# Hybrid streaming encoder layer: sample keys masked one turn ahead, and a re-laid order of the steps within a turn

## The chip, the cores and the metric

One NeuronCore of one Trainium2 chip runs the whole program. The metric is the device time of one launch in microseconds (us). Engines are named as in the profile: PE (matmul), DVE (vector), ACT (scalar), POOL (GpSimd), SP (the queue that issues most DMAs). Each engine runs its own list of instructions strictly in the order in which it was written, and waits on semaphores; whatever stands behind a waiting instruction waits too.

## The reference

One layer of a streaming encoder over 1024 prompt tokens and 8 sample streams of 16 tokens. After a combined input projection there are two head groups: sparse attention (8 heads) and a gated delta rule (8 heads, chunks of 64). The part that the change concerns is the delta rule of a head, for the prompt and for the samples:

```python
a_mat = jnp.where(strict, jnp.einsum('bnhid,bnhjd->bnhij', kb, k) * decay, 0.0)
m_mat = a_mat + jnp.eye(chunk, dtype=f32)
sol = lax.linalg.triangular_solve(m_mat, rhs, left_side=True, lower=True, unit_diagonal=True)
u, w = sol[..., :DV], sol[..., DV:]
kd = k * jnp.exp(glast[..., None] - gc)[..., None]

def step(s, inp):
    u_n, w_n, qg_n, qk_n, kd_n, gl_n = inp
    v_new = u_n - jnp.einsum('bhcd,bhde->bhce', w_n, s)
    o = jnp.einsum('bhcd,bhde->bhce', qg_n, s) + jnp.einsum('bhij,bhje->bhie', qk_n, v_new)
    s = s * jnp.exp(gl_n)[..., None, None] + jnp.einsum('bhcd,bhce->bhde', kd_n, v_new)
    return s, o
```

and afterwards `o` is normalised per token, gated with SiLU(z) and goes to the output projection. The 8 samples have a state each, and their 8 x 16 tokens share one tile of 128 rows, so the update `kd^T v_new` has to be cut by sample.

## The kernel before

The program has stages one after the other: normalise the input, project (and select keys) in 61 blocks, prepare gates, then `run_heads`, then the attention of the samples, then the output projection. The change lies in `run_heads` alone, which takes some 870 us of the 3215.

`run_heads` works on three heads at a time. `whole_order` lists ten iterations (turns), i = -2 to 7; in turn i the chain of states of head i runs (steps M_ and S_ and O_), the solve and the attention of head i+1 (D_, A_), and convolution and norms of head i+2 (N_). `iteration(i)` gives every step a place between 0 and 1 with `spread(first, last, steps)` and sorts by it; every engine's `run` then emits, in that one sorted order, its own part of each step. So the numbers in `iteration` are not times: they fix the order in which each engine takes its work, and nothing else.

What a turn does, with the names that the prediction uses:

- **M_read, M_state** (8 tiles): PE multiplies with the state S, DVE forms `vn` and updates S and `o`. A strict chain from tile to tile. DVE's memset of S (L1498) begins it, and stands for the turn's start here.
- **S_state, S_turn, S_new, S_out**: the samples. PE multiplies the 8 states (L1366), ACT copies that out, PE turns it back, DVE forms `vn_sample` (L1514), ACT writes the first part of `o` (in S_new), PE adds the second part (L1377, into PSUM) and DVE sums both (L1519). Then POOL multiplies `vn_sample` by a mask of the samples into `vmask`, eight copies side by side (L1060), and PE multiplies `kd^T vmask` into two PSUM banks (L1381), which DVE adds to the sample states (L1522). L1381 waits for the mask and also for `o_ready`, that is for L1519.
- **O_square, O_norm, O_out**: ACT squares `o`, DVE sums and normalises, ACT takes the root between (L1189), DVE scales `o` (L1532), PE turns it in three groups (L1391).
- **D_keys** (POOL: keys and values times gates, then clears TU), **D_turn, D_gram** (gram matrices with decays, five pairs of tiles; DVE writes A), **D_out, D_base, D_back**: SP sends the 16x16 diagonal blocks of A to memory and back in another layout; POOL forms first the masked levels Bm (L1039, four multiplies), then inverts the blocks (30 small steps, `base`); SP brings the inverses back into TU with eight DMAs. **D_level** (8 levels of matmuls, PE L1293 is the first of each), **D_last**, **D_solve** (uw, for the next turn).
- **N_tap, N_conv, N_silu** (convolution of head i+2, nine DVE passes L1442, then SiLU on ACT), **N_turn** (nine tiles turned on PE, L1237), **N_squares, N_sum, N_norms, N_unit** (unit norms; their result starts the next turn's D_keys and D_turn).
- **A_logits, A_bias, A_exp, A_norm, A_turn_p, A_values, A_gate**: attention of head i+1 in 12 parts, 8 tiles of queries.

The shared buffer `vmask` carries three things one after the other: the copy of the sample state (`swq`, its first two tiles), the mask product, and the squares of `o`. ACT needs a table load when it changes between Exp, SiLU and Sqrt.

## Time and profile before

| | us |
|---|---|
| three runs: median | 3215.42 |
| three runs: lowest, highest | 3193.49, 3221.22 |
| profiled execution, its time | 3217.03 |
| its span (first to last instruction) | 3214.9 |
| PE / DVE / ACT / POOL busy over the span | 87% / 36% / 30% / 26% |
| mean granted clock of PE over the span | 0.918 |

The page of the profile cuts the span into 40 slices. PE is busy nine tenths or more in the projection and in the output projection, and between four and eight tenths in slices 23 to 33, where `run_heads` lies; there DVE and ACT are each busy about half of the time. A row of the timeline reads: start in us from the span's start, duration, engine, source line, operation, output <- inputs, shapes, count; a bracket at its end gives how long the engine stood idle before it and who ended that. Several equal instructions may be merged into one row (x4).

### The profile page before, as it was taken

What the parts mean: (1) busy time and instruction counts of PE and PEld (TensorE: products, weight loads), DVE (VectorE), ACT (ScalarE), POOL (GpSimd) and SP (SyncE); (2) the same over time, 40 slices, a digit from 0 to 9 for tenths busy, and PEclk for the clock granted to TensorE, in tenths of its full rate; (3) what the DMA queues carried; (4) which work ended last, traced back from release to release, by engine and by line L of the source; (5) the groups of instructions that cost most, each with busy time, mean ns of one, the idle gap of its engine ahead of it and who ended that gap; (6) DMA issues with size and microseconds to landing.
All of it is one profiled execution on the core that took longest, in us unless ns stands there. A gap on an engine that the chain in (4) does not pass through costs nothing. (4 is left out here: it accounts for less than half of the span.)

```text
span 3214.9 us, 39925 instructions
## 1 busy us (share of the span) xinstructions
PE 2807.4 (87%) x15333; PEld 2503.0 (78%) x15333; DVE 1163.1 (36%) x2044; ACT 957.4 (30%) x1662; POOL 844.0 (26%) x713
## 2 busy tenths in 40 slices
PE   4999899999999999999999458777777685799997
PEld 3999599798989989899999437666566563487875
DVE  7000100843818062250600256555665542304142
ACT  5111111313121121211211344655556542222221
POOL 6222012121211212112122132232331320255553
PEclk6999699999999989999999779988898895699998
DMA  3222122121221212222121411222122113446543
GB/s 130 66 64 64 39 64 73 49 69 54 65 68 53 72 50 63 67 65 73 59 64 59 139 49 46 68 77 60 37 67 68 55 42 84 166 145 221 169 177 124
DMA packets 301720, 259.02 MB, mean 81 GB/s; under 512 B 88232, under 2 KB 252176, under 8 KB 299152
## 3 DMA queue, kind: packets, MB, share of 16 engines
q1 hardware_dynamic: 291564, 212.35, 22.5%
q10 hardware_dynamic: 10048, 45.27, 3.5%
q8 instruction: 63, 1.03, 0.1%
q14 instruction: 45, 0.37, 0.0%
HBM read 192.25 MB, written 65.33 MB: 80 GB/s over the span
## 5 line engine op out<-in xcount | busy, mean ns | idle before, releaser
L394 PE MATMUL bank<-hH,wL 128*128 128x384 f32 (+1 forms) x2928 | 981.9, 335 | 14.9 <-POOL wL L311 14.9
L395 PE MATMUL bank<-hL,wH 128*128 128x384 f32 (+1 forms) x2928 | 980.5, 335 | 0.0
L396 PE MATMUL bank<-hH,wH 128*128 128x384 f32 (+1 forms) x2928 | 980.2, 335 | 0.0
L311 POOL TENSOR_TENSOR wL<-raw,wH 128x512 fp32r<-128x512 f32 x244 | 314.2, 1288 | 1390.3 <-ACT wH L328 1390.3
L394 PEld LDWEIGHTS bank<-hH,wL 128*128 128x128 f32 (+1 forms) x2928 | 550.3, 188 | 19.2 <-issue 18.5
L395 PEld LDWEIGHTS bank<-hL,wH 128*128 128x128 f32 (+1 forms) x2928 | 550.3, 188 | 0.8
L396 PEld LDWEIGHTS bank<-hH,wH 128*128 128x128 f32 (+1 forms) x2928 | 550.2, 188 | 0.7
L328 ACT ACTIVATE wH<-raw 128x512 fp32r<-128x512 f32 x244 | 154.2, 632 | 1020.2 <-PE bank L396 964.6
L1902 POOL TENSOR_TENSOR owL<-oraw,owH 128x2048 fp32r<-128x2048 f32 x48 | 225.5, 4699 | 268.2 <-ACT owH L1922 268.2
L506 DVE TENSOR_SCALAR score<-relued,w_idx 128x512 f32<-128x512 f32 (+3 forms) x10 | 7.8, 778 | 685.1 <-ACT relued L353 684.6
L1961 PE MATMUL ob<-owH,mL 128*128 128x512 f32 x576 | 227.8, 395 | 28.6 <-POOL owL L1902 28.6
L1962 PE MATMUL ob<-owL,mH 128*128 128x512 f32 x576 | 226.5, 393 | 0.0
L1963 PE MATMUL ob<-owH,mH 128*128 128x512 f32 x576 | 226.3, 393 | 0.0
L471 DVE MAX8 top<-score 128x8 f32<-128x1024 f32 (+6 forms) x200 | 175.3, 877 | 6.9
L339 ACT ACTIVATE ptbuf<-bank 128x384 f32<-128x384 f32 (+1 forms) x183 | 90.1, 492 | 288.4 <-PE bank L396 288.4
L472 DVE MATCH_REPLACE8 score<-top,score 128x1024 f32<-128x1024 f32 (+6 forms) x200 | 171.6, 858 | 0.0
L1922 ACT ACTIVATE owH<-oraw 128x2048 fp32r<-128x2048 f32 x48 | 91.8, 1914 | 236.0 <-PE ob L1963 215.2
L1961 PEld LDWEIGHTS ob<-owH,mL 128*128 128x128 f32 x576 | 109.6, 190 | 55.4 <-issue 31.8
L1963 PEld LDWEIGHTS ob<-owH,mH 128*128 128x128 f32 x576 | 109.5, 190 | 23.2
L1962 PEld LDWEIGHTS ob<-owL,mH 128*128 128x128 f32 x576 | 109.7, 190 | 22.5
L446 PE MATMUL bank<-region 64*128 64x512 f32 (+3 forms) x320 | 118.1, 591 | 6.1 <-ACT relued L353 5.9
L1442 DVE SCALAR_TENSOR_TENSOR y<-xc,keep_cw,y 128x1179 f32<-128x1179 f32 x72 | 113.0, 1572 | 11.2 <-ACT y L1069 9.9
(302 smaller groups left out, 3457.2 us busy)
## 6 DMA issues: line engine op xcount, KB each, us to landing
raw<-in_w_in SPq DMA_DIRECT2D x240, 256.0 KB, 2.8
oraw<-in_w_out SPq DMA_DIRECT2D x48, 1024.0 KB, 5.1
proj_scratch<-ptbuf ACTq DMA_DIRECT2D x60, 576.0 KB, 2.8
xc<-proj_scratch SPq DMA_DIRECT2D x8, 1536.0 KB, 7.7
mraw<-mix_scratch SPq DMA_DIRECT2D x12, 768.0 KB, 5.8
x<-in_x_prompt SPq DMA_DIRECT2D x8, 1024.0 KB, 4.8
out_y_prompt<-yv ACTq DMA_DIRECT2D x8, 1024.0 KB, 4.0
ox<-in_x_prompt SPq DMA_DIRECT2D x8, 768.0 KB, 6.6
```

The costliest lines, as they stand in the source:

```text
L311: pool.tensor_tensor(wL[c % 2][:, :, :], raw[c][:, :, :], wH[c % 2][:, :, :].bitcast(F32), ALU.subtract).then_inc(low_ready, 1)
L328: nc.scalar.activation(wH[c % 2][:, :, :], raw[c][:, :, :], ACT.Copy).then_inc(high_ready, 1)
L394: pe.matmul(o, low, hH[:, kk, tok], start=first, stop=False)
L395: pe.matmul(o, high, hL[:, kk, tok], start=False, stop=False)
L396: last = pe.matmul(o, high, hH[:, kk, tok], start=False, stop=end)
L446: pe.matmul(rel[u % BANKS_REL][:, 0:width], qi[i % 2][rows, hd // 2, :], kiT[rows, c:c + width], start=True, stop=True).then_inc(rel_done, 1)
L471: chain(nc.vector.max(top8[:, :], sc))
L472: chain(nc.vector.match_replace(out=sc, in_to_replace=top8[:, :], in_values=sc, imm_value=TAKEN))
L1902: pool.tensor_tensor(wL[n % 2][:, :, :], raw[n % 2][:, :, :], wH[n % 2][:, :, :].bitcast(F32), ALU.subtract).then_inc(low_ready, 1)
L1961: pe.matmul(o, mL[:, kk, a], wH[n % 2][:, k, :], start=first, stop=False)
L1962: pe.matmul(o, mH[:, kk, a], wL[n % 2][:, k, :], start=False, stop=False)
L1963: last = pe.matmul(o, mH[:, kk, a], wH[n % 2][:, k, :], start=False, stop=end)
```

## The change

The sample mask no longer multiplies `vn_sample`, late in the chain of its own turn, but the keys `kd` of the samples, in the turn before: step S_keys, on POOL, writes `kd_seg`. PE then multiplies each sample's masked keys with `vn_sample`: eight matmuls of 128 columns with stationary operands of their own, in place of two of 512 columns with one. `swq` gets a buffer of its own. On POOL the levels Bm move behind the inversion of the blocks. And the places in `iteration` are set anew: grams end at 0.22 instead of 0.26, states run to 0.42 instead of 0.36, samples and output steps follow closer, attention is stretched from 0.74 to 0.80, the levels lie at 0.56 to 0.80 instead of 0.55 to 0.86, N_turn ends at 0.80 and the norms lie at 0.80 to 0.95 instead of 0.90 to 1.0. DMA steps move with them; the load of x for head i+3 goes from 0.78 to 0.52.

```diff
-        placed += spread(0.0, 0.36, states) + spread(0.36, 0.52, sample) + spread(0.52, 0.66, out)
+        placed += spread(0.0, 0.42, states) + spread(0.42, 0.50, sample) + spread(0.50, 0.62, out)
...
-        placed += spread(0.66, 0.90, natural) + spread(0.90, 1.0, norms)
+        placed += spread(0.62, 0.80, natural) + spread(0.80, 0.95, norms)
...
-        vmask = sbt("vmask", [P, TILES, P])
+        kd_seg = sbt("kd_seg", [P, TILES, P])
         wq = sbt("wq", [P, DEC_B, 2, DEC_T])
-        swq = vmask[:, 0:2, :]
+        swq = sbt("swq", [P, 2, P])
...
                 def base(h, _k):
-                    wait(pool, a_ready, h, 5)
-                    for m in range(LEVELS):
...
                     wait(pool, blocks_in, h, 16)
                     w = base_w[:, 0, :, :]
...
                     pool.tensor_copy(base_w[:, 1, :, :], w.rearrange("p r c -> p c r")).then_inc(base_done.sem, 1)

-                def sample_mask(h, _k):
-                    wait(pool, sm_vn, h, 1)
-                    pool.tensor_tensor(vmask[:, 0:DEC_B, :], vn_sample.unsqueeze(1).to_broadcast([P, DEC_B, P]), K["segcol"][:, :].unsqueeze(2).to_broadcast([P, DEC_B, P]), ALU.mult).then_inc(sm_mask.sem, 1)
+                    wait(pool, a_ready, h, 5)
+                    for m in range(LEVELS):
+                        if m == 0:
+
+                            wait(pool, wt_done, h - 1, NS)
+                        for g in range(2):
+                            lo, hi = QUADS[g]
+                            pool.tensor_tensor(Bm[m][:, lo:hi, :], A[:, lo:hi, :], K["level"][:, m, :].unsqueeze(1).to_broadcast([P, hi - lo, P]), ALU.mult).then_inc(level_ready.sem, 1)
+
+                def sample_keys(h, _k):
+                    wait(pool, o_norms, h - 1, 1)
+                    wait(pool, sm_ds, h - 1, 3)
+                    pool.tensor_tensor(kd_seg[:, 0:DEC_B, :], kd[h % 2][:, NT, :].unsqueeze(1).to_broadcast([P, DEC_B, P]), K["segcol"][:, :].unsqueeze(2).to_broadcast([P, DEC_B, P]), ALU.mult).then_inc(sm_mask.sem, 1)
...
                     for half in range(2):
-                        pe.matmul(big[:, half, :], kd[h % 2][:, NT, :], vmask[:, 4 * half:4 * half + 4, :], start=True, stop=True).then_inc(sm_ds.sem, 1)
+                        for b in range(4):
+                            last = pe.matmul(big[:, half, b * P:(b + 1) * P], kd_seg[:, 4 * half + b, :], vn_sample, start=True, stop=True)
+                        last.then_inc(sm_ds.sem, 1)
```

**POOL, from the end of one inversion to the start of the next.** In these rows `de` are the blocks being inverted, `kbe`, `kd` and `vb` the keys and values of D_keys. Before:

```order
L1056 COPY de<-de 72x256
L1060 TENSOR_TENSOR vmask<-uw,keep_segcol 128x1024
L1023 TENSOR_TENSOR kbe<-nat,keep_gates 128x1152
L1024 TENSOR_TENSOR kd<-nat,keep_gates 128x1152
L1025 TENSOR_TENSOR vb<-nat,keep_gates 128x1152
L1029 MEMSET TU 128x2304
L1039 TENSOR_TENSOR Bm<-AQ,keep_level 128x512 x4
L1042 TENSOR_SCALAR de<-de 72x256
```

and now:

```order
L1048 COPY de<-de 72x256
L1057 TENSOR_TENSOR Bm<-AQ,keep_level 128x512 x4
L1062 TENSOR_TENSOR kd_seg<-kd,keep_segcol 128x1024
L1023 TENSOR_TENSOR kbe<-nat,keep_gates 128x1152
L1024 TENSOR_TENSOR kd<-nat,keep_gates 128x1152
L1025 TENSOR_TENSOR vb<-nat,keep_gates 128x1152
L1029 MEMSET TU 128x2304
L1034 TENSOR_SCALAR de<-de 72x256
```

The four multiplies for Bm went from ahead of the inversion to behind it, and the masking reads `kd` where it read `uw`.

**ACT, around the sample step, in a full turn.** `vmask`/`swq` in the first row is the copy of the sample state, `PT` an attention tile, `uw` with `keep_gates` the first part of `o` (the last such row is that of S_new), `y` the SiLU of the convolution (N_silu). Before:

```order
L1069 ACTIVATE vmask<-big 128x8x2x16
L1069 ACTIVATE PT<-big 128x512
L1069 ACTIVATE uw<-big,keep_gates 128x128
L1085 ACT_TABLE_LOAD
L1085 ACTIVATE y<-y 128x1024
L1069 ACTIVATE PT<-big 128x256
L1085 ACTIVATE y<-y 128x1024 x2
```

and now:

```order
L1071 ACTIVATE swq<-big 128x8x2x16
L1071 ACTIVATE PT<-big 128x512
L1087 ACT_TABLE_LOAD
L1087 ACTIVATE y<-y 128x1024 x2
L1071 ACTIVATE uw<-big,keep_gates 128x128
L1199 ACTIVATE zb<-zb 128x1152
L1087 ACTIVATE y<-y 128x1024
```

The copy of S_new moved behind a table load and two SiLUs.

**ACT, from the squares of `o` to the root.** `osq` is the root of O_norm, `lg` a row of attention logits (A_exp). Before:

```order
L1202 ACT_TABLE_LOAD
L1202 ACTIVATE lg,am<-lg,am 128x896
L1197 ACT_TABLE_LOAD
L1197 ACTIVATE zb<-zb 128x1152
L1185 ACTIVATE vmask<-uw 128x1152
L1189 ACT_TABLE_LOAD
L1189 ACTIVATE osq<-osq 128x9
```

and now:

```order
L1195 ACTIVATE za<-za 128x1024
L1187 ACTIVATE kd_seg<-uw 128x1152
L1204 ACT_TABLE_LOAD
L1204 ACTIVATE lg,am<-lg,am 128x896
L1191 ACT_TABLE_LOAD
L1191 ACTIVATE osq<-osq 128x9
```

An exponential with a table load of its own moved from ahead of the squares to between the squares and the root; one table load fewer stands in the piece.

## Rows read from the trace of the kernel before

**Rows 1.** Busy time by stretch; columns: stretch, length, each engine's busy time, clock, DMA.
```profile
1960.64:2561.47 600.83, 454.83 (x2988) 378.86 (x2988) 355.02 (x740) 331.50 (x654) 185.43 (x240) 0.89 0.21 59
...
2561.47:2643.91 82.44, 64.62 (x429) 53.89 (x429) 40.56 (x107) 34.49 (x78) 24.58 (x40) 0.90 0.15 41
```

**Rows 2.** Tile S (ns min/median/max, first to last start); timeline of DVE, two turns' starts.
```profile
L1498 DVE MEMSET S<- x8: 165/165/165, 1960.6 to 2643.9; 128x128 f32 x8
...
2161.80 0.17 DVE L1498 MEMSET S<- 128x128 f32 x1
...
2261.00 0.17 DVE L1498 MEMSET S<- 128x128 f32 x1
```

**Rows 3.** Timeline of PE in turn i = 2; its last row is turn i = 7.
```profile
2203.62 2.08 PE L1366 MATMUL big<-wq,Ss 128*128 128x32 f32 x16
...
2208.91 0.49 PE L1377 MATMUL big<-uw,AQ 128*128 128x128 f32 x2 [0.29 <-DVE uw L1514]
...
2217.92 3.55 PE L1381 MATMUL big<-vmask,kd 128*128 128x512 f32 x4 [8.53 <-POOL vmask L1060]
...
2224.24 0.61 PE L1293 MATMUL big<-TU,Bm 128*128 128x128 f32 x4
...
2227.04 0.66 PE L1391 MATMUL big<-ident,uw 128*128 128x128 f32 x4 [2.19 <-DVE uw L1532]
...
2251.16 0.55 PE L1237 MATMUL big<-ident,y 128*128 128x128 f32 x3
...
2669.57 3.78 PE L1381 MATMUL big<-vmask,kd 128*128 128x512 f32 x4 [1.18 <-POOL vmask L1060]
```

**Rows 4.** Line L1060, who waited for it: who, us in total, times.
```profile
  PE big L1381: 55.4, 8
```

**Rows 5.** Timeline of POOL in turn i = -1, then i = 2, then i = 6.
```profile
1895.64 8.61 POOL L1039 TENSOR_TENSOR Bm<-AQ,keep_level 128x512 f32<-128x512 f32 x4 [18.88 <-DVE AQ L1474]
...
2168.09 2.02 POOL L1029 MEMSET TU<- 128x2304 f32 x1
...
2192.87 7.47 POOL L1039 TENSOR_TENSOR Bm<-AQ,keep_level 128x512 f32<-128x512 f32 x4 [22.76 <-DVE AQ L1474]
...
2215.41 0.60 POOL L1056 COPY de<-de 72x256 f32<-72x256 f32 x1
...
2215.97 1.89 POOL L1060 TENSOR_TENSOR vmask<-uw,keep_segcol 128x1024 f32<-128x1024 f32 x1
...
2591.93 5.21 POOL L1039 TENSOR_TENSOR Bm<-AQ,keep_level 128x512 f32<-128x512 f32 x4 [22.15 <-DVE AQ L1474]
...
2598.55 0.85 POOL L1042 TENSOR_SCALAR de<-de 72x256 f32<-72x256 f32 x1 [1.41 <-DMA de<-base_a_scratch]
```

**Rows 6.** Timeline of ACT in turn i = 2.
```profile
2207.46 0.60 ACT L1069 ACTIVATE PT<-big 128x512 f32<-128x512 f32 x1 [1.35 <-PE big L1414]
...
2208.88 0.37 ACT L1069 ACTIVATE uw<-big,keep_gates 128x128 f32<-128x128 f32 x1 [0.82 <-DVE uw L1514]
...
2209.27 1.28 ACT L1085 ACT_TABLE_LOAD   x1
...
2211.79 1.99 ACT L1085 ACTIVATE y<-y 128x1024 f32<-128x1024 f32 x2
...
2216.45 1.04 ACT L1202 ACTIVATE lg<-lg,am 128x896 f32<-128x896 f32 x1
...
2221.57 1.16 ACT L1185 ACTIVATE vmask<-uw 128x1152 f32<-128x1152 f32 x1 [1.51 <-PE big L1381]
...
2252.63 2.12 ACT L1104 ACTIVATE y<-nat 128x2304 f32<-128x2304 f32 x1
```

**Rows 7.** Line L1442 (min/median/max ns); timeline of DVE in turn i = 2.
```profile
L1442 DVE SCALAR_TENSOR_TENSOR y<-xc,keep_cw,y x72: 1435/1442/2562, 1837.2 to 2507.1; 128x1179 f32<-128x1179 f32 x72
...
2167.72 2.44 DVE L1435 COPY xc<-keep_cw 128x72 f32<-128x72 f32 x1
...
2225.62 1.36 DVE L1532 TENSOR_TENSOR uw<-uw,osq 128x1152 f32<-128x1152 f32 x1 [0.28 <-ACT osq L1189]
```

More of the change, by code:

```diff
@@ L782, in iteration @@
         solves = [("D_solve", h, g) for g in range(5)]
-        placed += spread(0.0, 0.07, turns) + spread(0.07, 0.26, grams) + [(0.265, ("D_out", h, 0)), (0.29, ("D_base", h, 0)), (0.42, ("D_back", h, 0))]
-        placed += spread(0.55, 0.86, levels) + spread(0.86, 0.92, [("D_last", h, q) for q in range(3)]) + spread(0.92, 1.0, solves)
+        placed += spread(0.0, 0.05, turns) + spread(0.05, 0.22, grams) + [(0.225, ("D_out", h, 0)), (0.24, ("D_base", h, 0)), (0.38, ("D_back", h, 0)), (0.57, ("S_keys", h, 0))]
+        placed += spread(0.56, 0.80, levels) + spread(0.80, 0.86, [("D_last", h, q) for q in range(3)]) + spread(0.88, 0.98, solves)
         attend = []
@@ L1031, in base @@
                 def base(h, _k):
-                    wait(pool, a_ready, h, 5)
-                    for m in range(LEVELS):
-                        if m == 0:
-                            wait(pool, wt_done, h - 1, NS)
-                        for g in range(2):
-                            lo, hi = QUADS[g]
-                            pool.tensor_tensor(Bm[m][:, lo:hi, :], A[:, lo:hi, :], K["level"][:, m, :].unsqueeze(1).to_broadcast([P, hi - lo, P]), ALU.mult).then_inc(level_ready.sem, 1)
                     wait(pool, blocks_in, h, 16)
@@ L1170, in sample_state @@
                     wait(act, sm_done, h, 1)
-                    copy(swq.rearrange("p n (b t) -> p b n t", b=DEC_B), big[:, 0, 0:2 * P].rearrange("p (b n t) -> p b n t", b=DEC_B, n=2)).then_inc(sm_out.sem, 1)
+                    copy(swq[:, :, :].rearrange("p n (b t) -> p b n t", b=DEC_B), big[:, 0, 0:2 * P].rearrange("p (b n t) -> p b n t", b=DEC_B, n=2)).then_inc(sm_out.sem, 1)
                 def state(h, t):
@@ L1184, in square @@
                     wait(act, sm_ds, h, 3)
-                    do(vmask[:, :, :], o, ACT.Square).then_inc(o_squares.sem, 1)
+                    do(kd_seg[:, :, :], o, ACT.Square).then_inc(o_squares.sem, 1)
                 def out_root(h, _k):
```

22 lines of the change are left out of this document (11 added, 11 removed).

## Prediction

> **What bounds the kernel now.** I read the stretches first. `run_heads` has eight memsets of S, one at the start of each turn i = 0 to 7, from 1960.6 to 2643.9 [rows 2]; six full turns lie between 1960.64 and 2561.47, 600.83 us or 100.1 each, and turn 6 takes 82.4 [rows 1]. In the full turns PE is busy 455 of 601 us, DVE 355, ACT 332, POOL 185: no engine is full, so a turn is as long as its longest chain through the five fixed lists, and a stall counts only if it lies on that chain.
>
> Next the timeline of PE in turn i = 2, which runs from 2161.80 to 2261.00 [rows 2]. S_state ends at 2205.70 (2203.62 + 2.08), the first part of the sample output starts at 2208.91, and then PE stands 8.53 us until 2217.92, for POOL's mask [rows 3]. All eight such waits sum to 55.4 us [rows 4]. POOL's timeline says why the mask is late: it ran 2215.97 to 2217.86, directly behind the last step of the inversion (2215.41 + 0.60); the inversion began when the four Bm multiplies ended at 2200.34, and those began at 2192.87, when the last gram was written [rows 5]. The mask stands in POOL's list behind work it has nothing to do with. Behind PE's wait stand L1381, D_level's first matmul at 2224.24 and O_out at 2227.04, again after 2.19 us of waiting [rows 3]; from O_out PE has work to the last N_turn, which ends at 2251.71, and 9.3 us later the next turn starts [rows 2, 3]. So the chain of a turn today is: grams, Bm, inversion, mask, L1381, squares, norm, O_out, levels with N_turn, norms of head i+2, next turn.
>
> **The change, step by step, for a full turn.** I put the times against the end of S_state, s = 2205.70.
>
> (1) *The mask leaves the chain.* L1381 then waits for L1519 only, and L1519 for ACT's copy in S_new. Today that copy stands directly behind an attention copy (2208.88); now a table load and two SiLUs come first. From s: the hand-off, the copy of the sample state and the attention tile (0.60, ending 2.4 after s today, about 1.35 when PE turns that tile right behind S_state), table load 1.28, two SiLUs 1.99, the copy 0.37 [rows 6], DVE's sum and the hand-off about 0.3. That is 5.3 after s, bounded by 4.9 and 6.3. Today L1381 starts 12.2 after s. Gain 6.9. A new wait of about 2 to 3 us on PE stays, ended by ACT.
>
> (2) *The mask itself* is the same size (128 x 1024) on POOL, 1.89 us [rows 5], now behind Bm and long before its use in the next turn: nothing, covered by POOL's idle time (it is busy 185 of 601 us [rows 1]). Without that cover it would cost 1.89.
>
> (3) *L1381 itself*: 2 matmuls x 512 columns become 8 x 128, the same 1024 columns (each runs as two passes), but with a weight load for each. No row shows this shape. Below it stands L1366, sixteen passes with own weights in 2.08 us, above it today's 3.55 [rows 3]; I take 3.55, no change, since columns and passes are equal and PE comes out of a wait as it does now.
>
> (4) *From L1381 to O_out.* Today 9.12 us (2217.92 to 2227.04) [rows 3]. Now an Exp with its table load stands on ACT between the squares and the root: L1381 3.55, squares 1.16, load 1.28, Exp 1.04, load 1.28, then root, the scaling on DVE 1.36 [rows 3, 6, 7] and hand-offs of about 0.7 give 10.4. Cost 1.3, bounds 0 (if ACT reaches the Exp early) and 2.3 (load and Exp in full).
>
> (5) *s moves.* DVE's list now puts convolutions 6 and 7 ahead of the last M_state instead of behind it: 2 x 1.44. Against it, today one convolution beside the Bm multiplies took 2.56 instead of 1.44 [rows 7], which goes as Bm moves behind the convolutions. Net +1.8; the grams are packed earlier, which lets M run a little freer; I take +1.2, bounds 0 and 3.
>
> (6) *The other chain, grams to levels.* With Bm out of the way the inversion starts when its blocks have come back. Turn 6 shows that time: Bm starts 2591.93, the inversion at 2598.55 after waiting 1.41 us for the DMA: 6.6 instead of 7.5 [rows 5]. Then the inversion as now, 15.7 (2200.34 to 2216.01), and at most 8.2 to the first level (2216.01 to 2224.24) [rows 3, 5]: grams + 30.5. If the grams ended no earlier than now (31.1 into the turn), the first level could start 61.6 in; by (1) to (5) O_out, which stands ahead of it in PE's new list, starts 65.2 - 6.9 + 1.3 + 1.2 = 60.8 in. So this chain follows close behind. Three fewer half-steps of M and one convolution fewer stand ahead of the last gram in the new lists; I expect the grams 1 to 3 us earlier, which makes O_out the later one. Bm runs beside the DMAs that bring the inverses back, 5.2 to 7.5 against 8.2.
>
> (7) *O_out to the last N_turn*: 24.7 today. The new list has one logits part, one turn and one level more behind O_out, and gets rid of short waits of about the same sum. Zero, bounds +-1.5.
>
> (8) *The border.* Norms still begin with the squares behind the last N_turn, since N_turn stands between the levels on PE. The new lists put D_last's copy ahead of the squares (2.12 [rows 6]) and one of D_last's subtractions between the sums: +0.7, bounds 0 and 2.1. N_pads goes ahead of the first update of S. Today this small copy took 2.44 us in turn 2, until POOL's memset of TU was over (2168.09 + 2.02) [rows 5, 7]. In the new place it would wait for the same end: nothing more, since in most turns the scaling ahead of it is held to that end already.
>
> (9) *DMAs.* The load of x is issued some 20 us earlier, behind the inverses and the sample store; its reader comes only in the next turn. The waiting SP holds back only stores. Zero. `swq` in its own buffer: zero.
>
> Sum for a full turn: -6.9 + 1.3 + 1.2 + 0 + 0.7 = -3.7; I take **-3.4**, since (6) is near. Turn 6 has no SiLUs and no norms but the chain of (6) alone; I give it the same. Turn 7 loses its wait of 1.18 [rows 3]; turn -1 starts its inversion up to 2.0 earlier (Bm took 8.61 there against 6.6 [rows 5]), I take 1.5. Together 7 x 3.4 + 1.2 + 1.5 = 26.5 us. The profiled execution took 3217.0 (span 3214.9 and 2.1 around it), 1.6 more than the median of 3215.4: 3190.5 for it, **3189** against the median.
>
> **Two rules of the Trainium skill.** Of table loads the rows show 1.28 us: the load ends at 2210.55 and the second SiLU starts at 2211.79 [rows 6], so one SiLU of about 1.0 lies between and nothing more. The Trainium skill's page "ScalarE: Activation LUTs", section "What ACT_TABLE_LOAD costs", adds a drain of 1.38 us to each load. By the page, (4) would be 2 x 1.38 = 2.8 us dearer, and the time 7 x 0.6 + 2.7 = 7 us below today's, 3208. The trace does not agree, as there is no room for a drain; I give that no chance of its own. The other rule is the second rival's.
>
> **Rivals.**
> *A: the whole wait comes back.* s doesn't move, the exponential is not in the way and the grams end 3 us earlier: 6.5 a turn, 7 x 6.5 + 2.7 = 48 us, 3167. For it: the mask wait is the one long stall of PE, and turn 6's Bm at 5.21 shows that POOL is faster when undisturbed [rows 5]. Against it: (4) and (6).
> *B: POOL holds DVE in O_norm.* Bm (5.2 to 7.5) and the new mask 1.89 now run directly behind the inversion, while DVE normalises `o` with a small scaling from SBUF to SBUF. The copy of N_pads, 2.44 us until POOL's run ended, is such a hold [rows 5, 7]. If the scaling is held to the mask's end, the turn loses about 1.9 more: -1.5, in all 13 us, 3202. The Trainium skill's page "SBUF — State Buffer", section "Who interferes with whom", says that DVE's two-port modes and POOL lock each other out for a whole instruction; N_pads agrees. Against: the root waits for ACT's table load anyway, some 1.5 us.
> *C: slower.* The states are stretched from 0.36 to 0.42 of the turn. If S_state's end followed its place, it would go from 43.9 in (2205.70 - 2161.80) to 51.2, 7.3 later instead of 1.2: +2.7 a turn, 7 x 2.7 - 2.7 = 16 us, 3231. It decides from 4.6 later on (3.4 + 1.2). Against: DVE's work ahead of it grows by 1.8, no more.
>
> **How the numbers follow.** Forecast (3175 to 3203) 0.50, A 0.26, B 0.14, C 0.10. About 1% (32 us, 3183) is what a measurement of this kernel can tell from no change. Faster by over 1%: A and a third of the forecast, 0.42. Slower by over 1% needs C with a shift of 9 and more: 0.06. Within 1%: 0.52. The range leaves out the far half of A and most of C: 3156 to 3212.
>
> **What would show it.** L1381's successor starts 5 to 6 us after S_state, released by ACT or DVE and not POOL; the inversion starts 6.6 after the last gram; O_out about 61 into the turn; about 10 from the last N_turn to the next memset; turns of 96 to 97. I am wrong if S_state ends later than 47 in, if DVE's scaling in O_norm shows a duration far over 0.2, or if PE waits for the inverses rather than for O_out.

## The result, and the profile after

The changed kernel takes 3174.4 us (median of 4 runs, 3163.9 to 3179.5), the kernel before 3208.7 in the runs beside it: ratio 0.9867, with a 95% interval of 0.9842 to 0.9893 (the quotient of the two medians is 0.9893, the upper end of it). It is 1.1 to 1.6% faster; the forecast was 3189 with "within 1%" as the likeliest case. The direction is right, the time lies in the range of 3156 to 3212, and the wait for the mask went as forecast. But the gain is larger, because the forecast had one term with the wrong sign: S_state's end, which came earlier and not later.

The profiled execution has a span of 3174.0 against 3214.9. The stretches of the changed kernel's trace that answer to [rows 1] (the six full turns, then turn 6; columns as there):

```profile
1958.18:2528.55 570.37, 457.78 (x3042) 393.28 (x3060) 347.62 (x741) 320.97 (x649) 165.60 (x241) 0.89 0.22 62
2528.55:2605.01 76.46, 61.10 (x438) 51.95 (x441) 43.14 (x106) 35.67 (x80) 24.10 (x40) 0.93 0.16 43
```

Six turns take 570.37 instead of 600.83, 95.1 instead of 100.1 each: 5.1 less, where 3.4 was forecast. Turn 6 is 6.0 shorter, also for 3.4. PE is busy as long as before (458 and 455): nothing was saved, only waiting.

PE in turn i = 2 of the changed kernel, which runs from 2148.54 to 2244.13 (start, duration, engine, line, tiles, idle time before and what ended it); the rows answer to [rows 3]:

```profile
2189.11 1.94 PE L1368 MATMUL big<-wq,Ss 128*128 128x32 f32 x16 [0.85 <-DVE S L1512]
...
2192.82 0.39 PE L1379 MATMUL big<-uw,AQ 128*128 128x128 f32 x2
2196.26 2.69 PE L1384 MATMUL big<-uw,kd_seg 128*128 128x128 f32 x16 [3.05 <-DVE uw L1523]
...
2206.61 1.11 PE L1395 MATMUL big<-ident,uw 128*128 128x128 f32 x4 [5.36 <-DVE uw L1536]
2207.52 1.06 PE L1295 MATMUL big<-TU,Bm 128*128 128x128 f32 x4
...
2231.39 0.49 PE L1239 MATMUL big<-ident,y 128*128 128x128 f32 x3
...
2235.24 1.11 PE L1325 MATMUL big<-WT,TU 64*64 64x64 f32 x8 [1.61 <-ACT WT L1071]
2236.86 0.79 PE L1338 MATMUL big<-vb,TU 128*128 128x128 f32 x2 [0.51 <-DVE TU L1497]
2237.45 0.63 PE L1339 MATMUL big<-TU,kbe 128*128 128x128 f32 x2
```

S_state ends at 2191.05 (2189.11 + 1.94), 42.5 into the turn. The main sample matmul (L1384) follows 5.2 later, released by DVE's sum and not by POOL: the wait of 8.53 in [rows 3] is gone, one of 3.05 is left. But before O_out (L1395) PE now stands 5.36. Over the whole program the waits for that scaling of `o` are the largest of this stretch (who waited at line L1395: who, us in total, times):

```profile
  DVE uw L1536: 89.2, 16
```

(L1395 is counted twice there, for its matmuls and for its weight loads; half of it, 45 us, is PE's.)

The table puts the segments of a turn side by side, as means over the six full turns, in us from the memset of S, the turn's start. Each is read from the timelines' rows: last gram written, end of S_state, start of the main sample matmul, start of O_out, start of the first level, end of the last N_turn, next memset.

| | grams | S_state's end | sample matmul | O_out | first level | N_turn's end | turn |
|---|---|---|---|---|---|---|---|
| before | 32.4 | 45.3 | 57.5 | 66.7 | 64.0 | 90.8 | 100.1 |
| after | 27.1 | 42.5 | 47.9 | 58.0 | 58.9 | 83.3 | 95.1 |
| segment, measured | -5.2 | -2.8 | -6.8 | +0.9 | | +1.2 | +2.5 |
| segment, forecast | -1 to -3 | +1.2 | -6.9 | +1.3 | | 0 | +0.7 |

(The segments run from S_state's end to the sample matmul, O_out, the last N_turn and the next memset: -2.8 - 6.8 + 0.9 + 1.2 + 2.5 = -5.0, and -5.1 without rounding.) Two terms lie outside their bounds: S_state comes 4.0 earlier than forecast, and the border from N_turn to the next turn costs 1.8 more.

### The profile page after: what moved, and what is told of

Its sections match the earlier page's. It is cut to its first block and busy times, and to the rows that moved or that the text cites. A ratio compares the mean times of both kernels' runs of the same rounds, so it can differ in the third digit from the quotient of the medians.

```text
span 3174.0 us, 40095 instructions
## 1 busy us (share of the span) xinstructions
PE 2804.9 (88%) x15405; PEld 2516.8 (79%) x15429; DVE 1156.2 (36%) x2044; ACT 948.0 (30%) x1657; POOL 819.6 (26%) x713
## 5 line engine op out<-in xcount | busy, mean ns | idle before, releaser
L1965 PE MATMUL ob<-owH,mL 128*128 128x512 f32 x576 | 227.0, 394 | 28.6 <-POOL owL L1906 28.6
L1993 DVE TENSOR_TENSOR yv<-ob,ox 128x512 f32<-128x512 f32 x36 | 22.6, 685 | 257.6 <-PE ob L1967 257.6
```

Of the source, the lines that this page charges most:

```text
L1965: pe.matmul(o, mL[:, kk, a], wH[n % 2][:, k, :], start=first, stop=False)
```

## Each part alone, and two parts undone

All figures are means over six full turns of the profiled execution, as in the table; ratios are to the kernel before, run beside each (its medians there were 3212 to 3218). Total times carry chance: two executions of the one changed kernel are 19 us apart (1826.6 and 1807.2) already at the first copy of N_pads, where `run_heads` has only begun. So the turns are compared first. The code changes are shown shortened: `...` stands for what is left out, and words behind `#` explain and are not in the code.

**The mask's step alone.** The kernel before, with the old table and Bm ahead, takes the keys' mask, the eight small matmuls and `swq`:

```
-  "S_new": sample_mask          # vmask = vn_sample x segcol, behind the inversion
+  "S_keys": sample_keys         # kd_seg = kd x segcol, at 0.57 of the turn before
```

> The kernel before with the mask step alone: keys masked in their own step ahead of time (kd_seg, S_keys at 0.57, 8 matmuls of 128 columns, swq apart), the old table of places, Bm ahead of the inversion as before. Theory T (the mask's gain needs the earlier grams): POOL's mask no longer stands between S_state and the main sample matmul, which starts 3.5 to 5.5 us behind S_state's end instead of 12.2; but the grams end where they did (32.4 into a turn), so the first level stays at about 64, and O_out, which stands behind it on PE, moves only from 66.7 to 65 to 66. Turns 1 to 2 us shorter, in all 8 to 14 us: 3195 to 3201 beside 3208.7. Rival R (the mask carries the gain alone): O_out 5 us earlier, turns of 95, 3174.

Measured 3208.6, ratio 0.9988 (0.9967 to 1.0009). The sample matmul comes 5.1 behind S_state, yet the way from there to O_out takes 15.7 instead of 9.2: O_out at 64.8. PE in its turn i = 2 says why:

```profile
2208.64 2.94 PE L1384 MATMUL big<-uw,kd_seg 128*128 128x128 f32 x16 [0.47 <-DVE uw L1523]
...
2222.18 1.22 PE L1295 MATMUL big<-TU,Bm 128*128 128x128 f32 x4 [3.92 <-DMA TU<-base_w_scratch]
```

The next wait is 3.92 us for the inverses coming back by DMA. The mask's wait, the longest of PE, was worth 0.5 us of a turn by itself, less than theory T's 1 to 2 and far from rival R's 5: the other chain (grams, inversion, levels) lay directly behind it.

**The new table alone**, with the old mask behind the inversion and Bm ahead of it:

> The new table of places alone: the mask stays on the sample's values behind the inversion, Bm ahead of the inversion, 2 matmuls of 512 columns, as before. Theory T: grams end at 27 into a turn, the inversion ends 7.5 + 15 later at 49.7, mask 1.9, main sample matmul at 52 instead of 57.5, O_out at 62, last N_turn 25 later, border 11.8: turns of 99, 1 us shorter than before, about 7 us in all: 3202. If the order carries the gain alone (rival O): turns of 95, 3174. If it gives nothing without the mask's step (rival R): 3207 to 3212.

Measured 3207.5, ratio 0.9973 (0.9949 to 0.9998). Grams at 26.4, inversion to 49.9, sample matmul at 51.8, O_out at 62.1, turns of 99.0: the theory's numbers. Neither part is measured at more than 0.3% alone; both together make 0.8% (the next run, where only Bm's move is missing), and with Bm's move 1.3%.

**Bm back ahead of the inversion**, everything else as changed:

```
+                    wait(pool, a_ready, h, 5)
+                    for m in range(LEVELS):          # the four Bm multiplies
...
                     wait(pool, blocks_in, h, 16)     # inversion
...
-                    wait(pool, a_ready, h, 5)
-                    for m in range(LEVELS):
```

> The changed kernel with the four Bm multiplies put back ahead of the inversion. Theory T: the inversion starts about 1 us later behind the grams, the first level at 60 instead of 58.9, O_out unmoved at 58 or a little earlier, since in turns 2, 4 and 6 DVE's small scaling in O_norm (2.72, 2.13 and 5.77 us instead of 0.17) is no longer held by Bm: within 5 us of the changed kernel either way, 3170 to 3179. Rival S (S_state came early because Bm no longer runs beside the convolutions): S_state's end 1.5 to 3 us later in each turn, time 3185 to 3195.

Measured 3187.1, ratio 0.9919 (0.9892 to 0.9945). Rival S is right: grams at 26.9, nearly as in the changed kernel (27.1), but S_state's end at 44.9 instead of 42.5. DVE, then POOL, in its turn 2:

```profile
2182.17 2.21 DVE L1446 SCALAR_TENSOR_TENSOR y<-xc,keep_cw,y 128x1179 f32<-128x1179 f32 x1
...
2184.49 1.36 DVE L1573 TENSOR_SCALAR lg<-lg,am 128x640 f32<-128x640 f32 x1
...
2186.43 1.79 DVE L1446 SCALAR_TENSOR_TENSOR y<-xc,keep_cw,y 128x1179 f32<-128x1179 f32 x1
```

```profile
2181.87 7.48 POOL L1039 TENSOR_TENSOR Bm<-AQ,keep_level 128x512 f32<-128x512 f32 x4 [19.59 <-DVE AQ L1478]
```

Beside Bm (2181.87 to 2189.35) a convolution takes 2.21 and the next 1.79 instead of 1.44, and the small scaling of the attention 1.36 instead of 0.55 (both in the changed kernel). The forecast had counted one convolution of 2.56 [rows 7].

**The grams at their old places**, everything else as changed:

```
-  spread(0.0, 0.05, turns) + spread(0.05, 0.22, grams) + [(0.225, D_out), (0.24, D_base), (0.38, D_back), ...
+  spread(0.0, 0.07, turns) + spread(0.07, 0.26, grams) + [(0.265, D_out), (0.29, D_base), (0.42, D_back), ...
```

> The changed kernel with D_turn, D_gram, D_out, D_base and D_back at their old places (0 to 0.07, 0.07 to 0.26, 0.265, 0.29, 0.42), all else as changed. Theory T (grams packed into the first fifth are what moves both the levels and S_state): grams end at 31 to 32, the first level at 62 to 63, O_out no longer the later one; S_state's end back at 44 to 45; turns 2.5 to 4 us longer than the changed kernel's 95.1, 3192 to 3200. Rival S (S_state came early through Bm's move or the convolutions' places): S_state's end stays at 42 to 43, turns longer by 2.5 at most through the levels.

Measured 3211.1, ratio 0.9993 (0.9977 to 1.0009): the whole gain is gone. Grams at 33.0, S_state's end at 45.7, O_out at 62.5. But a row of DVE, 4.06 into its turn 2, spoils the reading:

```profile
2160.06 4.12 DVE L1573 TENSOR_SCALAR lg<-lg,am 128x128 f32<-128x128 f32 x1
2162.15 2.08 DVE L1439 COPY xc<-keep_cw 128x72 f32<-128x72 f32 x1
```

A_norm's scaling of 128 x 128 takes 0.29 in the changed kernel and 4.12 here (3.7 to 4.1 in every turn). That hold is looked at below, and this run repeated without it.

## What bounds the turn of the changed kernel

**The state chain unstretched.**

```
-  spread(0.0, 0.42, states) + spread(0.42, 0.50, sample)
+  spread(0.0, 0.36, states) + spread(0.38, 0.52, sample)
```

> The changed kernel with the state chain back in the first 0.36 of a turn (sample from 0.38 to 0.52), so that each half-step stands ahead of a convolution or a gram that it now follows. Theory T (stretching the states did cost S_state some 4 us, as rival C had it, and packed grams and the move of Bm paid for it): S_state's end at 38 to 40 instead of 42.4, the grams 0.5 to 1.5 later, O_out held by the squares' chain or the inverses: turns within 1.5 us, 3165 to 3182. Rival: the stretch cost nothing; S_state stays at 42 to 43.

Measured 3190.3, ratio 0.9930 (0.9893 to 0.9968): slower than the changed kernel. S_state's end came at 41.3, only 1.2 earlier, and the grams at 28.6. A_norm's first scaling was held 3.7 in every full turn here too, and O_norm's 4.2 to 5.2. Neither side's number came out, so this run doesn't price the stretch.

**D_last ahead of the squares at the border.** This looks at the 11.8 us from the last N_turn to the next memset, 9.3 before. Turn 2 from O_out to the last N_turn, and from there to the next memset, for the kernel before and then for the changed one (windows, columns as in [rows 1]):

```profile
2227.04:2251.71 24.67, 23.24 (x184) 21.34 (x185) 10.47 (x20) 11.05 (x23) 0.00 (x0) 0.93 0.50 144
2251.71:2261.00 9.29, 6.37 (x63) 5.96 (x63) 6.66 (x9) 7.09 (x12) 0.00 (x0) 1.00 0.31 114
```

```profile
2206.61:2231.88 25.27, 24.60 (x186) 22.41 (x188) 10.49 (x22) 11.30 (x24) 0.00 (x0) 0.91 0.57 167
2231.88:2244.13 12.25, 9.82 (x72) 9.21 (x71) 7.57 (x14) 7.45 (x13) 0.51 (x1) 0.72 0.11 43
```

The border ran at full clock (1.00) before; after, 0.72 was granted. ACT's timeline of the changed kernel has the squares of N_squares ahead of D_last's second copy (WT):

```profile
2232.81 2.12 ACT L1106 ACTIVATE y<-nat 128x2304 f32<-128x2304 f32 x1
2234.83 0.36 ACT L1071 ACTIVATE WT<-big 64x256 f32<-64x256 f32 x1
```

PE waits 1.61 for that copy (the row of 2235.24 above), and D_solve's products of two passes then take 0.63 (the row of 2237.45): granted 0.50 from 2235.24 to 2241.71, the lower of the two clock levels, 1.2 GHz, which begins in that wait. In the next run, where PE doesn't wait there, they take 0.39, at 2.4 GHz (granted 1.00). But turn 5 of the changed kernel has the same wait of 1.61, and there the clock stayed up:

```profile
2518.71:2528.55 9.84, 7.14 (x72) 6.56 (x71) 7.39 (x14) 7.23 (x13) 0.12 (x1) 1.00 0.14 55
```

So with the wait and the full clock the border takes 9.8, 0.5 more than before; in the other five turns it takes 11.4 to 12.5, granted 0.72 to 0.85, and some 2 of the 2.5 is the clock. Why it fell in five borders and not in the sixth, no run shows.

```
-  spread(0.80, 0.86, [("D_last", h, q) for q in range(3)])  ...  spread(0.80, 0.95, norms)
+  spread(0.800, 0.806, [("D_last", h, q) for q in range(3)])  ...  spread(0.807, 0.94, norms)
```

> The changed kernel with D_last's three parts ahead of N_squares on ACT and DVE (places 0.800 to 0.806, norms from 0.807). Theory T (the border is 11.8 us and not 9.3 because the squares, 2.12 us, stand ahead of D_last's second copy, and D_solve ends after the norms): PE's wait of 1.61 us ahead of D_last's second product goes, D_solve starts 1.5 us earlier, N_turn's end to the next memset 9.8 to 10.5; six borders, 8 to 12 us: 3163 to 3167. Rival N (the norms are the later chain): border 11.3 or more, 3171 to 3175.

Measured 3177.4, ratio 0.9883 (0.9837 to 0.9930). PE at the start of D_solve in its turn 2:

```profile
2233.60 0.49 PE L1338 MATMUL big<-vb,TU 128*128 128x128 f32 x2 [0.51 <-DVE TU L1497]
2233.93 0.39 PE L1339 MATMUL big<-TU,kbe 128*128 128x128 f32 x2
```

The border fell to 10.2, as theory T has it, but for another reason: PE now stands 2.05 a little later, for ACT's copy of `uw`, and what is gained is the clock (0.94 to 1.00 in all six borders). Yet the time did not follow: S_state's end went from 42.5 to 43.5, and turn 6 from 76.5 to 81.4, where A_norm's scaling was held 4.18.

**The SiLUs behind O_norm.** ACT in turn 2 of the changed kernel has no gap from 2191.56 to 2204.15: table load, SiLUs, squares, table load, exponential, table load. Three of its rows:

```profile
2195.37 0.35 ACT L1071 ACTIVATE uw<-big,keep_gates 128x128 f32<-128x128 f32 x1
...
2199.25 1.16 ACT L1187 ACTIVATE kd_seg<-uw 128x1152 f32<-128x1152 f32 x1
...
2204.95 0.21 ACT L1191 ACTIVATE osq<-osq 128x9 f32<-128x9 f32 x1 [0.80 <-DVE osq L1534]
```

```
-  spread(0.45, 0.49, gates) ...  (0.47, O_silu)
+  spread(0.54, 0.56, gates) ...  (0.5395, O_silu);  A_bias part 9 at 0.4695, A_exp 6 at 0.4705
```

> The changed kernel with ACT's SiLUs (N_silu, A_silu, O_silu) behind O_norm, and the logits' part 9 and exponential 6 next to S_new, so that no SiLU and only one table load stand on ACT between S_state and the root. Theory T (ACT bounds the stretch from S_state to O_out, and the inverses stand close behind): main sample matmul 3 to 3.5 behind S_state instead of 5.6, O_out 4 to 5 earlier, 53 to 54 into the turn; the first level then waits for the inverses until 57.5 to 59, so turns shrink by 1 to 2 only: 3160 to 3167. Rival A (O_out alone bounds, the inverses have room): turns shrink by 4: 3146. Rival Z (the late SiLUs hold up the first levels' copies on ACT): same or slower, 3174 to 3185.

Measured 3167.4, ratio 0.9853 (0.9800 to 0.9907). The sample matmul comes 4.0 behind S_state, but O_out only at 57.1, 11.7 behind the matmul instead of 10.1. DVE and POOL of its turn 2:

```profile
2194.85 1.35 DVE L1533 TENSOR_REDUCE osq<-kd_seg 128x9 f32<-128x1152 f32 x1
2196.24 2.83 DVE L1535 TENSOR_SCALAR osq<-osq 128x9 f32<-128x9 f32 x1
```

```profile
2192.24 4.94 POOL L1060 TENSOR_TENSOR Bm<-AQ,keep_level 128x512 f32<-128x512 f32 x4
2197.13 1.90 POOL L1065 TENSOR_TENSOR kd_seg<-kd,keep_segcol 128x1024 f32<-128x1024 f32 x1
```

O_norm's scaling of 128 x 9 numbers lasts 2.83 (5.33 in four of the six full turns) and ends when POOL's S_keys ends, at 2199.03. That is rival B's mechanism, and here it is the bound (the run that splits Bm, below, takes most of it away and has O_out 3.1 earlier than the same kernel without the split).

**S_keys later.** In the changed kernel itself O_norm's scaling lasted 2.72, 2.13 and 5.77 in turns 2, 4 and 6, else 0.17.

```
-                    wait(pool, o_norms, h - 1, 1)
+                    wait(pool, o_norms, h - 1, 3)
```

> The changed kernel, where POOL's S_keys waits for the third step of O_norm (the reciprocal) instead of the first, so that it can't run while DVE's small scaling stands there. Theory B (the scaling is held by POOL's run of Bm and S_keys): its duration, 2.72, 2.13 and 5.77 us in turns 2, 4 and 6 of the changed kernel and 0.17 in the others, falls to 1.0 at most in turns 2 and 4, and to 3.9 in turn 6, where Bm itself still holds it; ACT's root then waits 0.8, 0.35 and 1.9 us less: 3 us in all, 3170 to 3175, too little for the time and read in the trace. Rival: the long scalings have another cause; then they stay.

Measured 3174.2, ratio 0.9879 (0.9832 to 0.9927). The scaling took 1.0 at most in the full turns and 3.97 in turn 6, where ACT's root waited 2.37 instead of 4.18. With Bm ahead of the inversion (the run above) it took 0.17 in all eight turns, though S_keys runs there too: the hold comes with Bm's new place.

**N_pads later; four moves; three moves.**

```
-  spread(0.03, 0.08, taps) + spread(0.08, 0.45, conv)
+  spread(0.093, 0.113, taps) + spread(0.113, 0.45, conv)
```

> The changed kernel with N_pads and the taps at 0.093 to 0.113 (behind M_state.1) instead of 0.03 to 0.08. Theory H (the small copy of N_pads on DVE is held until one of POOL's D_keys instructions ends, 2.12 us or 4.06 us from the same start, and the state chain and the grams stand behind it: grams at 25.3 or 27.2): the copy falls to 0.2 to 1.5 us, M_state.1 at 8.6 at the latest, grams at 25.5 or less in every turn; 1.5 to 2 us in most turns, 3160 to 3168. Rival V (another small instruction of DVE is held in its place, A_norm.1 above all): grams stay at 27, 3170 to 3178.

> The changed kernel with four small moves together: S_keys behind O_norm's reciprocal, D_last ahead of N_squares, SiLUs behind O_norm, N_pads behind M_state.1. Theory T (each has its place on the chain, and what the first three met alone was POOL's hold of DVE): grams at 25, DVE's scaling in O_norm under 1 us, O_out at 53 to 54, first level at 55.5 to 56.5 by the inverses, border 10.1: turns of 90 to 91.5 instead of 95.1, in all 25 to 32 us: 3142 to 3150. Rival (the gains overlap, or the inverses bind): turns of 93, 3160.

> As the one with four moves, without D_last ahead of N_squares. Theory T: border 11.8 instead of 10.1, turns 1.6 longer: 3152 to 3160. Rival V (without the later border, POOL's D_keys start 0.5 ahead of the memset and hold nothing; with it, they start later against the memset, hold DVE longer and give the border's gain back): this one is no slower than the one with four moves.

Measured 3175.6 (ratio 0.9896, 0.9838 to 0.9953), 3173.1 (0.9888, 0.9836 to 0.9940) and 3177.2 (0.9889, 0.9834 to 0.9945). With N_pads late the grams end at 25.3 to 25.7 in every turn, as theory H has it, but S_state's end is 43.4. The taps and convolutions stand later there, among the state steps; that this is why was not tried. With four moves five turns take 92.2 to 92.9 and one 97.6, and there A_norm's scaling was held 4.15. By the turns D_last's move is worth 2.1 (93.4 with it, 95.5 in the run of three moves, without it). But turn 6 takes 81.3 with it, where that scaling was held 4.15 again, and 76.8 without, and the two ratios don't tell the runs apart. So rival V is neither shown nor refuted. By the ratios none of the three beats the changed kernel. With four moves a hold took back part of the gain; with N_pads late the three small instructions took no more than 1.2 in a full turn, so there the reason is another and open.

## The hold of DVE by POOL

DVE's timeline of the changed kernel: the copy of N_pads in turn 2, O_norm's scaling in turn 2, the copy in turn 3:

```profile
2152.26 4.06 DVE L1439 COPY xc<-keep_cw 128x72 f32<-128x72 f32 x1
...
2201.95 2.72 DVE L1532 TENSOR_SCALAR osq<-osq 128x9 f32<-128x9 f32 x1
...
2247.84 2.12 DVE L1439 COPY xc<-keep_cw 128x72 f32<-128x72 f32 x1
```

The copy of 128 x 72 numbers starts 3.71 or 3.72 into both turns; it takes 4.06 in one and 2.12 in the other. POOL runs four instructions of about 2.1 back to back there (three multiplies of D_keys, then the memset of TU), and both ends are ends of such an instruction: of the memset in turn 2 and of the last multiply in turn 3.

```profile
2154.26 2.01 POOL L1029 MEMSET TU<- 128x2304 f32 x1
...
2247.76 2.13 POOL L1025 TENSOR_TENSOR vb<-nat,keep_gates 128x1152 f32<-128x1152 f32 x1
```

With 2.12 the grams ended at 25.6 (turn 3), with 4.06 at 27.2 to 28.2 (the other five). The Trainium skill, "SBUF — State Buffer", section "Who interferes with whom", says that copies and scalings of DVE can run in a mode that needs a port pair shared with GpSimd, which whoever issues first holds for a whole instruction; and that operations of DVE with two inputs from SBUF contend with a GpSimd instruction that reads SBUF, not with one that only writes it. The trace agrees on who is held. On how long it differs, and the measurement decides: the held instruction can lose again at the next boundary, and in turn 6 O_norm's scaling waited for the four Bm and S_keys (5.77 us).

**Three small instructions written on two tensors.**

```
-  V.tensor_copy(pads, rows)                         # N_pads
+  V.tensor_tensor(pads, rows, rows, ALU.max)
-  V.tensor_scalar(lg, lg, am, None, ALU.mult)       # A_norm, t < 2
+  V.tensor_tensor(lg, lg, am.to_broadcast([P, w]), ALU.mult)
-  V.tensor_scalar(osq1, osq0, 1.0 / HD, EPS, ...)   # O_norm
+  V.scalar_tensor_tensor(osq1, osq0, 1.0 / HD, eps, op0=ALU.mult, op1=ALU.add)
```

> The changed kernel, where three small instructions of DVE (N_pads' copy, A_norm's scaling of t = 0 and 1, O_norm's scaling) are written as instructions on two tensors (max of a tensor with itself, a product with a broadcast column, mean and EPS as a scalar-tensor-tensor); values as before. Theory H (only copies and scalings from SBUF to SBUF are held to the end of one of POOL's instructions; the convolutions, of two tensors, never were): the copy 0.2 to 0.4 us instead of 2.12 or 4.06, O_norm's scaling under 0.4 in every turn, grams at 23.4 to 24.5 in every turn as in turn 6, turns 2 to 3.5 shorter: 3150 to 3162. Rival V (the hold goes by time or memory, not by the kind of instruction): durations stay, 3170 to 3180. Rival W (the hold goes, but the chain behind it is set elsewhere): durations fall, grams at 25, turns within 1 us, 3168 to 3176.

Measured 3165.8, ratio 0.9836 (0.9804 to 0.9868). Turns of 93.3, S_state's end at 40.7, grams at 25.4 in every turn. The theory is half right. N_pads is now always held to the end of POOL's last multiply, 2.14, never longer (DVE, then POOL in turn 2); but O_norm's still lasted 2.94, 2.81 and 5.80 in turns 3, 4 and 6:

```profile
2145.09 2.14 DVE L1441 TENSOR_TENSOR xc<-keep_cw 128x72 f32<-128x72 f32 x1
...
2559.20 5.80 DVE L1536 SCALAR_TENSOR_TENSOR osq<-osq 128x9 f32<-128x9 f32 x1
```

```profile
2144.98 2.16 POOL L1025 TENSOR_TENSOR vb<-nat,keep_gates 128x1152 f32<-128x1152 f32 x1
2147.08 2.02 POOL L1029 MEMSET TU<- 128x2304 f32 x1
...
2558.20 4.93 POOL L1057 TENSOR_TENSOR Bm<-AQ,keep_level 128x512 f32<-128x512 f32 x4
2563.09 1.90 POOL L1062 TENSOR_TENSOR kd_seg<-kd,keep_segcol 128x1024 f32<-128x1024 f32 x1
```

At 2147.1 POOL goes over to a memset, whose row names no input, and DVE goes on; in O_norm POOL goes from one multiply to the next, and DVE waits for all of them (2559.20 + 5.80 = 2565.00, S_keys ends at 2564.99). So the hold is not gone, but on two tensors it ends where POOL comes to the memset. That the reading decides is what the page has; no run puts anything but a memset there.

> The changed kernel once more, unedited, beside the other two on the same chip: 3174, ratio to the kernel before 0.9867 with 0.984 to 0.989. A second profile shows which of its turns have the copy of N_pads at 2.12 and which at 4.06 us: 1 and 5 in the first; another split here would show that the two values are chance and not the turn's number.

The changed kernel again: 3174.3, ratio 0.9883 (0.9851 to 0.9915). In this profile two of six turns have the copy at 2.12 (turns 0 and 4), grams at 25.3 there and at 27.2 to 28.2 in the others: the two values are chance.

**The same in the kernel before.**

> The kernel before, with the same three small instructions written on two tensors and nothing else. Theory H (in four of its six full turns A_norm's first scaling was held 3.4 to 4.2 us, in the other two 0.3, and grams ended at 32.5 to 33.4 there instead of 31.0): all six turns like the two quick ones or quicker, grams at 31, turns of 99.2, 1.0 us shorter on average: 6 to 8 us in all. This says how much of the change's gain is hold and not order. Rival: the hold takes another small instruction, turns stay at 99 to 101.

Measured 3197.0, ratio 0.9948 (0.9934 to 0.9962): 0.5% without the change. S_state's end at 42.0 instead of 45.3, turns of 97.9. The gain of the change between the two kernels on two tensors is 4.6 a turn (97.9 to 93.3), beside 5.1 between the two as they were.

**Moves on top of it.**

> As the one with three unheld instructions, and with SiLUs behind O_norm and D_last ahead of N_squares. Theory H: grams at 24, O_out at 51 to 53 or as early as the inverses allow, border 10.1: turns of 89 to 91, 3135 to 3148. Rival W: turns of 92 to 93 as in the four moves, 3160 to 3173.

Measured 3157.2, ratio 0.9826 (0.9799 to 0.9852), turns of 92.8. O_norm's scaling was held in all six full turns, 2.2 to 6.3, and O_out came at 57.1, no earlier than without the moves (56.5). Then POOL's list alone was changed:

```
                     for m in range(LEVELS):
+                        if m == 1:
+                            wait(pool, o_norms, h - 1, 3)
...
-                    wait(pool, o_norms, h - 1, 1)     # S_keys
+                    wait(pool, o_norms, h - 1, 3)
```

> As the one with three unheld instructions and the late SiLUs and early D_last, and POOL's second half of Bm (m = 1) and S_keys wait for O_norm's reciprocal, so that only the first half of Bm (2.5 us) can run beside O_norm. Theory H (in that kernel O_norm's scaling still lasted 2.2 to 6.3 us, always to the end of POOL's S_keys): the scaling falls under 1 us, O_out comes at 53 to 54 instead of 57, and PE then waits for the inverses at the first level, 55.5 to 56.5 instead of 58: turns of 90.5 to 91.5 instead of 92.8; 3143 to 3152. Rival W (the levels wait for the later half of Bm, or the inverses come no earlier than 57.5): turns within 0.5 us, 3153 to 3160.

Measured 3148.0, ratio 0.9794 (0.9781 to 0.9807): 2.1% faster than before, and faster than the changed kernel. O_norm's scaling over all turns (min/median/max in ns), without and with the split:

```profile
L1539 DVE SCALAR_TENSOR_TENSOR osq<-osq x8: 170/4241/6257, 2008.0 to 2619.1; 128x9 f32<-128x9 f32 x8
```

```profile
L1541 DVE SCALAR_TENSOR_TENSOR osq<-osq x8: 168/170/1965, 2009.5 to 2608.8; 128x9 f32<-128x9 f32 x8
```

and PE at O_out (L1401) and the first level of turn 2 with the split:

```profile
2194.44 1.11 PE L1401 MATMUL big<-ident,uw 128*128 128x128 f32 x4 [6.17 <-DVE uw L1545]
2196.47 1.23 PE L1301 MATMUL big<-TU,Bm 128*128 128x128 f32 x4 [0.92 <-DMA TU<-base_w_scratch]
```

O_out comes at 53.9, turns are 91.0, and PE waits 0.92 for the inverses at the first level: now both chains end together. The theory's numbers were met, but for two scalings of 2.0 (turns 2 and 4), where the theory had under 1.

## How S_state's earlier end divides

> The changed kernel with grams at their old places, and with the three small instructions written on two tensors. In the run with old grams alone, A_norm's first scaling was held 3.7 to 4.1 us (0.3 in the changed kernel), so that its later S_state (45.7 against 42.4) mixes the packing with that hold. Beside the unheld changed kernel (S_state's end at 40.7, grams at 25.4, turns of 93.3): if the packing itself moves the state chain, S_state's end is 43 or later, turns 97 or more; if it was the hold, S_state's end is 40 to 42, grams at 29 to 31, and turns are 95 to 97 through the inverses alone.

> The changed kernel with Bm ahead of the inversion, and with the three small instructions written on two tensors. Beside the unheld changed kernel (S_state's end at 40.7): if Bm beside the convolutions costs the state chain what the run with Bm ahead suggested, S_state's end is 42.7 to 43.5 in every turn and O_out 1.5 to 2.5 later; if that 2.5 was hold at the start of the turn, S_state's end is 40.5 to 41.5. O_norm's scaling 0.2 in every turn, as nothing of Bm runs beside it.

Measured 3196.2, ratio 0.9935 (0.9909 to 0.9961), and 3173.1, ratio 0.9876 (0.9843 to 0.9908). With the three small instructions on two tensors:

| three small instructions on two tensors | grams | S_state's end | O_out | turn |
|---|---|---|---|---|
| before | 30.1 | 42.0 | 64.7 | 97.9 |
| changed | 25.4 | 40.7 | 56.5 | 93.3 |
| changed, grams at old places | 31.6 | 44.4 | 61.2 | 97.9 |
| changed, Bm ahead | 25.5 | 43.5 | 58.7 | 94.5 |

Undoing the packing of the grams alone loses the whole gain: turns of 97.9, as in the kernel before. It also puts S_state's end back by 3.7, and undoing Bm's move puts it back by 2.8.

The 3.7 is not packing alone. A_norm's scaling, though on two tensors, takes 1.8 to 2.2 in every turn of the run with old grams, and 0.30 in the changed kernel on two tensors (turn 2 of each, in this order):

```profile
2157.92 2.24 DVE L1578 TENSOR_TENSOR lg<-lg,am 128x128 f32<-128x128 f32 x1
...
2144.86 0.30 DVE L1578 TENSOR_TENSOR lg<-lg,am 128x128 f32<-128x128 f32 x1
```

What such a hold costs can be read in the kernel before on two tensors: its two turns with a scaling of 0.3 have S_state's end at 40.6 and 40.8, its four with 1.5 to 2.2 have it at 42.6 to 42.8. So some 1.9 of the 3.7 can be that hold, and the packing itself is worth 1.8 to 3.7, an estimate from these rows.

Packing and Bm's move would make 6.5 together, but between the kernels on two tensors S_state's end moves by 1.3 only (42.0 to 40.7). So the rest of the new table (states stretched to 0.42, convolutions and N_pads ahead of state steps) costs 5.2 if the parts add up. Without that hold on both sides it is 4.6: 1.8 and 2.8 against turns that end S_state at 40.7 before and after. These are differences, and no run shows the stretch by itself. Of the 2.8 by which S_state's end moved between the two kernels as they were, the other 1.5 is hold: writing on two tensors takes 3.3 off in the kernel before (45.3 to 42.0) and 1.8 in the changed one (42.5 to 40.7).

## Why the prediction was right or wrong

**What bounds, and (1), (2), (3): right.** The mask is off the chain, and the sample matmul starts 5.4 behind S_state (forecast 5.3), in turn 2 after a wait of 3.05 that DVE ends. That this alone is worth little, 0.5 a turn, fits (6), which has the other chain close behind. The mask's new place costs PE nothing that shows. L1384 took 2.69 in turn 2 (above), between the bounds of 2.08 and 3.55.

**(4) right:** +0.9 for +1.3, with the table load and the exponential where they were put.

**(5) wrong, and this is the step that failed.** S_state's end was to move by +1.2 and moved by -2.8. The term's two convolutions were set against one convolution beside Bm (1.1 us) and "a little" for the packed grams. Bm's move was worth 2.8, since a second convolution and a scaling lie beside it as well (rows of the run with Bm ahead), and the packing 1.8 to 3.7. The scaling stood in the trace of before too, in turn 2, with 1.36 instead of the changed kernel's 0.55:

```profile
2194.25 1.36 DVE L1569 TENSOR_SCALAR lg<-lg,am 128x640 f32<-128x640 f32 x1
```

The cost on the other side was mis-sized too, some 5 instead of 2.9: rival C's mechanism was probably there, at two thirds of its price, and was paid for. And the term has nothing for the hold of A_norm's scaling, though (8) names it ("held to that end already" in most turns). It lasted 3.4 to 4.2 in four of the six turns of before and 0.3 in the changed kernel, and holds make 1.5 of the 2.8. The forecast took turn 2, one of the two without it, as the measure of all.

**(6) right in kind, short in size.** The inversion starts 7.2 behind the grams (6.6 forecast, 7.5 before), the first level 31.8 behind them (30.5), where it stands behind O_out; in the run that splits Bm, where it waits for the inverses, it comes 30.2 behind them. Grams were 5.2 earlier, not 1 to 3. O_out is the later one, as forecast, and the levels follow it at once.

**(7) and (8): mis-sized.** O_out to the last N_turn costs 1.2, not 0: PE is busy 24.6 of 25.3 us there in turn 2 of the changed kernel and 23.2 of 24.7 before, so the additional parts had no waits to go into. The border costs 2.5, not 0.7. The prediction has D_last's copy ahead of the squares; in the new list only its first copy is, the second stands behind them, and PE stood 1.61 for it in all six turns. With the full clock that costs 0.5 (turn 5), near the 0.7. What the term lacks is the clock: in five of six borders a part of D_solve ran at the lower level. Early D_last took 1.6 of the 2.5 away.

**Rivals.** A (the whole wait back, 6.5 a turn) gave the nearer number, but not for its reasons: the exponential was in the way, and S_state moved. That 3167 lies nearer than 3189 is luck. B (POOL holds O_norm) came true in turns 2, 4 and 6, where the scaling took 2.72, 2.13 and 5.77; ACT's root waited 0.80, 0.35 and 4.18 for it, 5.3 in all, less than the 13 forecast for B, since in the other turns DVE came first.

**The sum.** The span fell by 40.9 where 26.5 was forecast. Of the 14.4 between, the six full turns make 10.1 (30.5 against 20.4) and turn 6 makes 2.6; the rest lies ahead of the first turn and behind the last.

## What to carry to other kernels

A long wait that one resource explains can still be worth nothing alone: ask which chain ends next behind it, and undo each half of a change before crediting either. Here the mask's step and the new table gave 0.1 and 0.3% alone, and the change without the packed grams gave nothing. When steps change places in one list for five in-order engines, count for every step on the chain what runs beside it and what stands ahead of it on all engines, in several turns and not in one, since a turn can have two lengths. Where POOL runs instructions back to back, look for small DVE instructions whose duration ends with POOL's, and give POOL a wait there or move its work: here the last such step (splitting Bm) was worth 1.8 us a turn.

## What the runs showed of the hardware

A DVE instruction of 128 x 9 numbers took 0.17, or up to 6.58 us (turn 6 with the states at 0.36) where it began while POOL ran its multiplies back to back. The same copy with the same start took 2.12 or 4.06. Written on two tensors it took 2.14, to where POOL went over to a memset, while O_norm's scaling, also on two tensors, was held to the end of the fifth multiply in a row (5.80). Convolutions on two tensors (1.44) were only slowed (1.79 to 2.56). PE's clock fell in five of the changed kernel's six borders (granted 0.72 to 0.85, products of 0.63) during or after a wait of 1.61, and stayed up in the sixth with the same wait (1.00, products of 0.39). With D_last early it was granted 0.94 to 1.00, though PE waited 2.05 there.
